# A first pass over 192 instead of 256 prompt tokens, and a second over 96 rows instead of 32

## The chip, the cores and the metric

The kernel runs on one core of one Trainium2 chip, as one program. The metric is device time in microseconds (us), the median over runs.

## The reference, cut to what matters

The kernel computes one step of a decoder layer for 256 prompt tokens and 32 sample tokens (8 sequences of 4). All arithmetic is float32. In short:

```python
qa, ka, va, qb, kc, vc, ks, vs, kw, vw, g = split(x @ w_in)         # 2048 -> 44 tiles of 128 columns, and gates
o_a = stick_breaking(qa, keys, values)                                # 8 heads, samples over 2048 paged positions
kcmp, vcmp = compress(kc, w1_k, w2_k), compress(vc, w1_v, w2_v)        # windows of 32 positions, stride 16
o_c, sel = attend(qb, kcmp, vcmp), top16(importance)                  # compressed branch picks blocks of 64
o_b = g0 * o_c + g1 * attend(qb, selected ks, vs) + g2 * attend(qb, window kw, vw)
h = layer_norm(ALPHA * x + concat(o_a, o_b) @ w_out)                  # w_out 2048 x 2048
q = (h @ w_query).reshape(T, 8 heads, 2, 128); s = q . sub_keys        # w_query 2048 x 2048
experts, gate = top16 of the sums of two top16 lists, softmax          # 128 experts for each token
y = layer_norm(ALPHA * h + sum(gate * gelu(u[expert] . h) * v[expert]))  # rows of 2048 values, gathered
```

Each of the 288 tokens needs 128 rows of `peer_u` and 128 rows of `peer_v`, 8 KB each: 604 MB in all.

## The kernel before, in words

**Three stages.** First, 44 tiles of `w_in` are projected for all tokens, with stick-breaking attention of samples and prompt around it. Then a first pass applies `w_out` to the 256 prompt tokens in two tiles of 128 rows (`out_rows`, L1336), normalises them, turns them (`turn_prompt`, L1347) and applies `w_query` (`query_rows`, L1378; 16 blocks of 128 query columns, with `score_rows`, L1366). Then comes the gather stage, a loop of ticks.

**Slots and groups.** The tokens form 9 groups of 32. A slot is one group with four experts for each token: a gather of 128 rows of `peer_u` (1 MB), a dot product with the replicated `h` on VectorE (`gather_dot`, L2302), a gather of 128 rows of `peer_v`, and four matmuls of 32 output rows each on TensorE (`value_rows`, L1660). There are 288 slots. `slot_group` and `slot_column` say which group and columns a slot has; the first 64 slots alternate groups 0 and 1 (four slots each), the others take a group's 32 slots in one go. The value part of slot s comes 22 ticks later (`LAG`).

**Ticks.** Every engine walks through ticks 0 to 309. At tick t VectorE does `selection(t)`, `background(t)`, then the dot product of slot t; ScalarE does replication, `background(t)`, and the diagonal of slot t-22; TensorE does `background(t)`, then `value_rows(t-22)`; GpSimd issues the `peer_u` gather of slot t and then the `peer_v` gather of slot t-22 (L2410). Both gathers have rings of four buffers, so GpSimd waits for the dot product of slot t-4 and for the matmuls of slot t-26, and for the choice of experts (`chosen`, `CHOSEN_BY`). The first `peer_v` gather also waits until the whole `w_query` pass is over, since its ring holds those weights. Each engine's stream is in order: whatever waits in `background(t)` holds all that follows on that engine. TensorE enters tick 0 only after the last `score` of the first pass.

**The samples' chain** lies in `background`, at ticks written out by hand. Compression: 32 items (`taps`, L1421, 1 MB of pages each, two buffers), three ticks apiece from ticks 20 and 72 (`TAPS_AT`); each pair ends in `cmp_sums` and `cmp_gelu` on VectorE. Picking of blocks from tick 82 (`PICK_AT`), selected and window attention of two halves from 123 and 157 (`NSA_AT`), `w_out` for the 32 samples at 198 to 213 (`OUT_AT`, `out_of`, L1574: four matmuls of 32 rows side by side, then folded), `w_query` for them at 230 to 261 (`QUERY_AT`, `query_of`, L1599: half a block a tick). SyncE loads the weight blocks again for this, 1 MB each, into two of four buffers, each after the block two before it was used. The 1 MB blocks for the items of compression come half from SyncE's queue and half from ScalarE's (`odd_pages`).

**Selection.** The top 16 lists of a head are made on VectorE in three parts (`head_part`), the expert numbers by `experts_head` or `experts_pair`, and `fold` lays them out by slot. First tile at ticks 0 to 44, second at 56 to 104, samples at 240 to 271.

Of the kernel before, what the change touches and what calls it, by code (L numbers as in the profile page):

```python
# [136 lines left out]
TAPS_AT = (20, 72)  # L137
TAPS = {TAPS_AT[kv] + 3 * i + piece: (kv, i, piece) for kv in range(2) for i in range(2 * NB) for piece in range(3)}


def item_ticks(after):

    return {TAPS_AT[kv] + 3 * i + 2 + after: (kv, i) for kv in range(2) for i in range(2 * NB)}


def stage_ticks(after):

    return {TAPS_AT[kv] + 6 * b + 5 + after: (kv, b) for kv in range(2) for b in range(NB)}

# [3 lines left out]
PICK_AT = 82  # L153
NSA_AT = (123, 157)
# [48 lines left out]
CHOSEN_BY = {0: 1, 8: 2, 16: 3, 32: 4, 48: 5, 64: 6, 96: 7, 128: 8, 160: 9, 192: 10, 224: 11, 256: 12, 264: 13, 272: 14, 280: 15}  # L203
# [105 lines left out]
def hybrid_step(nc, dram, outs):  # L309
    stream, later_items = Stream(), Background()  # L310
    with ExitStack() as ctx:
# [175 lines left out]
        vcmp = words(AT_PROJ + 4096, NB, NG * P)  # L487
# [13 lines left out]
        s_cmp = words(AT_PROJ + 3648, 2, P)  # L501
        imp = words(AT_PROJ + 3904, 2, NSEL)
        rank = words(AT_PROJ + 3970, 2, NSEL)
        out_parts = [words(AT_PROJ + 2080 + 512 * k, 512) for k in range(2)]
        p_slc_t = words(AT_H + 4096, NPAGE, P)
# [1986 lines left out]
```

## Time and profile before

| | |
|---|---|
| median of 3 runs | 2566.43 us (2564.66 to 2570.31) |
| the profiled execution | 2569.75 us, of which its span is 2567.9 us |
| TensorE busy | 1892.7 us (74%), mean granted clock 0.811 of 2.4 GHz |
| VectorE busy | 1248.5 us (49%) |
| DMA | 964.23 MB, mean 375 GB/s |
| matmuls of the first pass over `w_out` | 110.1 us (L1336) |
| matmuls of the first pass over `w_query` | 114.2 us (L1378) |

The span runs from the first to the last instruction. "Busy" of TensorE counts modelled ends of pipelined matmuls. One float32 matmul of the program is two MATMUL instructions in the profile. The granted clock is 1.0 at 2.4 GHz and 0.5 at 1.2 GHz.

### The profile page before, as it was taken

To read this page: it belongs to the slowest core of one execution; us is meant where nothing else is said; L and a number is where in the kernel's file an instruction comes from. 1 tells how busy PE (TensorE), PEld (TensorE's weight loads), DVE (VectorE), ACT (ScalarE), POOL (GpSimd) and SP (SyncE) were. 2 spreads that over 40 slices of the span, in tenths; PEclk is the share of its full clock that TensorE was granted. 3 is DMA by queue.
4 is the path that set the end of the run, shared out by engine and by line. 5 is a ranking of instruction groups with operands and counts; after the bars stand their busy time and mean duration, and the time that the engine had idled before them with its cause. 6 is when DMAs were issued, how large, how long until landed. Compare 5 with 4: busy or idle time off the path is not lost.

```text
span 2567.9 us, 29141 instructions
## 1 busy us (share of the span) xinstructions
PE 1892.7 (74%) x9494; PEld 1077.5 (42%) x9494; DVE 1248.5 (49%) x2349; ACT 335.4 (13%) x787; POOL 709.9 (28%) x594
## 2 busy tenths in 40 slices
PE   8999999979999877757777663665553546888345
PEld 5777766544478654434454310221120002655000
DVE  0510122243048867677887535424433345578850
ACT  0000111422031000201100101101110110011011
POOL 0000000000002433333334324323434246334562
PEclk9999999989999998978988885787685655555556
DMA  9889979896349999999999999999999999999998
GB/s 397 301 344 357 371 278 376 339 363 263 121 182 361 391 408 410 408 411 412 409 409 410 410 397 410 409 397 398 415 386 395 421 422 421 421 421 411 419 417 326
DMA packets 213687, 964.23 MB, mean 375 GB/s; under 512 B 23937, under 2 KB 89474, under 8 KB 122818
## 3 DMA queue, kind: packets, MB, share of 16 engines
q0 software_dynamic: 84512, 627.05, 59.7%
q1 hardware_dynamic: 93074, 300.33, 30.6%
q10 hardware_dynamic: 35952, 35.01, 4.0%
q8 instruction: 76, 1.25, 0.2%
q14 instruction: 73, 0.60, 0.1%
HBM read 955.81 MB, written 14.88 MB: 378 GB/s over the span
## 4 chain that ended last, share of the span: by engine, by line
DMA 51%; PE 31%; DVE 9%; issue 4%; SPq 2%; POOL 1%; ACTq 1%; ACT 1%; POOLq 0%; DVEq 0%
DMA sb<-in_peer_u,sb 25%; DMA sb<-in_peer_v,sb 18%; PE bank L1030 14%; DVE sb L2302 5%; PE bank L1336 4%; DMA sb<-in_nsa_t 3%; DMA sb<-in_nsa_v 3%; PE bank L1660 2%; PE bank L1094 2%; PE bank L1134 2%; PE bank L1378 1%; DMA sb<-in_a_v 1%; POOL sb L2410 1%; PE bank L1486 1%; PE bank L1540 1%
## 5 line engine op out<-in xcount | busy, mean ns | idle before, releaser
L1660 PE MATMUL bank<-sb 128*32 128x512 f32 x2304 | 476.5, 848 | 535.6 <-DMA sb<-in_peer_v,sb 513.9
L2302 DVE CUSTOM_DVE_ANT_1 sb<-sb 128x2048 f32<-128x2048 f32 x224 | 513.5, 2293 | 522.5 <-DMA sb<-in_peer_u,sb 520.2
L2410 POOL DMA_INDIRECT sb<-in_peer_v,sb x288 | 400.7, 1391 | 462.5 <-PE bank L1660 380.5
L2410 POOL DMA_INDIRECT sb<-in_peer_u,sb x288 | 301.1, 1046 | 765.6 <-DVE sb L2302 530.5
L1660 PEld LDWEIGHTS bank<-sb 128*32 128x32 f32 x2304 | 63.3, 124 | 754.9 <-DMA sb<-in_peer_v,sb 714.9
L1030 PE MATMUL bank<-sb 128*128 128x288 f32 x1408 | 351.9, 410 | 11.7 <-DMA sb<-in_w_in 11.7
L1030 PEld LDWEIGHTS bank<-sb 128*128 128x128 f32 x1408 | 267.0, 191 | 95.5 <-issue 12.2
L1421 PE MATMUL bank<-sb 128*128 128x256 f32 x1024 | 289.6, 437 | 0.5 <-ACT sb L829 0.5
L1421 PEld LDWEIGHTS bank<-sb 128*128 128x128 f32 x1024 | 249.6, 309 | 79.7 <-issue 62.5
L2302 DVE CUSTOM_DVE_ANT_0 sb<-sb 128x2048 f32<-128x2048 f32 x64 | 146.6, 2294 | 78.6 <-DMA sb<-in_peer_u,sb 74.9
L996 ACT ACTIVATE sb<-sb 128x32 f32<-128x32 f32 x288 | 83.1, 313 | 509.8 <-PE bank L1660 284.8
L2396 POOL DMA_DIRECT2D out_a<-sb x1 | 0.5, 545 | 514.6 <-PE bank L1134 514.6
L1599 PEld LDWEIGHTS bank<-sb 128*128 128x128 f32 x512 | 111.6, 330 | 53.2 <-issue 53.2
L1486 PE MATMUL bank<-sb 128*32 128x512 f32 x128 | 78.9, 777 | 52.8 <-DMA sb<-in_nsa_t 52.8
L1599 PE MATMUL bank<-sb 128*128 128x32 f32 x512 | 116.0, 402 | 0.0
L1378 PE MATMUL bank<-sb 128*128 128x256 f32 (+1 forms) x608 | 114.2, 347 | 1.4 <-issue 0.7
L1336 PE MATMUL bank<-sb 128*128 128x512 f32 x256 | 110.1, 592 | 0.1
L1378 PEld LDWEIGHTS bank<-sb 128*128 128x128 f32 x608 | 99.8, 191 | 11.9 <-issue 0.9
L1540 PE MATMUL bank<-sb 128*32 128x256 f32 x256 | 75.0, 459 | 39.6 <-DMA sb<-in_nsa_v 39.6
L825 ACT ACTIVATE sb<-sb 32x2048 f32<-32x2048 f32 x36 | 68.6, 1906 | 68.2 <-issue 37.1
L667 ACT ACTIVATE sb<-bank 128x288 f32<-128x288 f32 x44 | 18.0, 410 | 440.0 <-PE bank L1030 440.0
L1336 PEld LDWEIGHTS bank<-sb 128*128 128x128 f32 x256 | 48.6, 190 | 61.1 <-issue 60.7
(363 smaller groups left out, 1489.2 us busy)
## 6 DMA issues: line engine op xcount, KB each, us to landing
sb<-in_a_k SPq DMA_DIRECT2D x128, 512.0 KB, 6.7
sb<-in_a_v SPq DMA_DIRECT2D x128, 512.0 KB, 6.8
sb<-in_w_in SPq DMA_DIRECT2D x44, 1024.0 KB, 9.0
sb<-in_w_out SPq DMA_DIRECT2D x32, 1024.0 KB, 8.9
sb<-in_w_query SPq DMA_DIRECT2D x32, 1024.0 KB, 9.1
sb<-in_nsa_t SPq DMA_DIRECT2D x200, 128.0 KB, 9.9
sb<-in_nsa_t ACTq DMA_DIRECT2D x184, 128.0 KB, 14.2
sb<-in_nsa_v SPq DMA_DIRECT2D x64, 128.0 KB, 18.2
```

Source lines behind the costliest of these rows:

```text
L825: act.activation(replica(g)[32 * q:32 * q + 32], src, ACT.Copy).then_inc(rep_in, 1)
L996: act.activation(diag[j % 4], const["fold"], ACT.Copy, scale=w16[:, r % 2, j:j + 1]).then_inc(diag_in, 1)
L1030: mm = pe.matmul(bank[step % 2][:, 0:T], w[:, kt * P:(kt + 1) * P], x_t[:, kt, :], start=(kt == 0), stop=(kt == KT - 1))
L1336: mm = pe.matmul(bank[3 * (n % 2) + tt][:, :], mix(4 * kq + kt)[:, P * tt:P * tt + P], w[:, kt, :], start=(kq == 0 and kt == 0), stop=(kq ...
L1378: mm = pe.matmul(bank[5 if m == 2 else m % 2][:, lo:hi], w[:, P * kt:P * kt + P], h_t[:, kt, lo:hi], start=(kt == 0), stop=(kt == KT - 1), ...
L1421: mm = pe.matmul(bank[(7, 3)[n % 2]][:, 0:256], rows[:, :, l], w1_one[:, :, l, :], start=(l == 0), stop=(l == 15), skip_group_check=True)
L1486: mm = pe.matmul(bank[((5, 6), (7, 2))[ph][c]][32 * b4:32 * b4 + 32, :], q_pad[:, 4 * h + b4, g], rows[:, 4 * c:4 * c + 4, g, :], start=(g ...
L1540: mm = pe.matmul(bank[4][r, 0:256], p_slc_t[:, 8 * ph + j, r], rows[:, 256 * j:256 * j + 256], start=(ph == 0 and j == 0), stop=False, ski ...
L1599: mm = pe.matmul(bank[2 + m % 2][:, 0:NSMP], w[:, P * kt:P * kt + P], h_t[:, kt, NPROMPT:T], start=(kt == 0), stop=(kt == KT - 1))
L1660: mm = pe.matmul(bank[g % 2][32 * c:32 * c + 32, :], diag[j % 4], v_ring[j % 4][:, 512 * c:512 * c + 512], start=(s in FIRST), stop=(s in ...
L2302: dve.tensor_tensor_reduce(out=u, in0=u, in1=replica(g), scale=1.0, scalar=0.0, op0=ALU.mult, op1=ALU.add, accum_out=act16[:, r % 2, j:j + ...
L2410: pool.indirect_dma_start(rows[j % 4], None, dram[table], bass.IndirectOffsetOnAxis(ap=idx, axis=0)).then_inc(full[j % 4], 16)
```

## The change: what it does

- The first pass takes 192 prompt tokens: tile 0 has 128 rows, tile 1 has 64 (`ROWS_1`). In `out_rows` for tile 1 the even and odd products go to rows 0 to 63 and 64 to 127 of the bank, and VectorE adds both. `score_rows` for tile 1 writes rows 64 to 127. `query_rows` streams 192 columns instead of 256.
- The other 64 prompt tokens and the 32 samples are tile 2 of 96 rows. `out_of` makes two products for each of 4 parts of a block, one of 64 rows and one of 32, in one bank; no fold. `query_of` takes a whole block in one tick, with 96 columns.
- Groups 0 to 5 are the first 192 tokens, 6 and 7 the other prompt tokens, 8 the samples. Slots 192 to 255 alternate groups 6 and 7.
- The chain: an item of compression starts every 2.25 ticks on average, from tick 6 on (in two pieces of 8 taps instead of three of 6, 6 and 4), picking at 50, attention at 80 and 114, `w_out` at 154 to 169, `w_query` at 178 to 193. The selection for tile 2 runs at ticks 183 to 218.
- The final norm of prompt tokens is in three parts, and the load of its weights waits for the last block of `w_query`.

```diff
+GROUPS_1 = 6
+ROWS_1 = NSMP * (GROUPS_1 - 4)
+TOK_1 = P + ROWS_1
+ROWS_2 = T - TOK_1
+ROWS_P = NPROMPT - TOK_1
+PARTS_1 = P // ROWS_1
...
-TAPS_AT = (20, 72)
-TAPS = {TAPS_AT[kv] + 3 * i + piece: (kv, i, piece) for kv in range(2) for i in range(2 * NB) for piece in range(3)}
+TAPS_AT = 6
+def taps_tick(kv, i):
+    n = 2 * NB * kv + i
+    return TAPS_AT + 9 * (n // 2) // 2 + 2 * (n % 2)
+TAPS = {taps_tick(kv, i) + piece: (kv, i, piece) for kv in range(2) for i in range(2 * NB) for piece in range(2)}
...
-    return {TAPS_AT[kv] + 6 * b + 5 + after: (kv, b) for kv in range(2) for b in range(NB)}
+    return {taps_tick(kv, 2 * b + 1) + 1 + after: (kv, b) for kv in range(2) for b in range(NB)}
...
-PICK_AT = 82
-NSA_AT = (123, 157)
+PICK_AT = 50
+NSA_AT = (80, 114)
-OUT_AT = 198
-QUERY_AT = 230
+OUT_AT = 154
+QUERY_AT = 178
+REPLICATE.update({192 + q: (7, q) for q in range(4)})
+def shared(s):
+    return s // 64 in (0, 3)
-CHOSEN_BY = {0: 1, 8: 2, 16: 3, 32: 4, 48: 5, 64: 6, 96: 7, 128: 8, 160: 9, 192: 10, 224: 11, 256: 12, 264: 13, 272: 14, 280: 15}
+CHOSEN_BY = {0: 1, 8: 2, 16: 3, 32: 4, 48: 5, 64: 6, 96: 7, 128: 8, 160: 9, 192: 10, 200: 11, 208: 12, 224: 13, 240: 14, 256: 15}
...
             def out_rows(k, tt):
                 n, kq = k // 4, k % 4
                 w = arrived("wo", k).rearrange("p (k c) -> p k c", k=4)
+                parts, rows = (1, P) if tt == 0 else (PARTS_1, ROWS_1)
                 for kt in range(4):
-                    mm = pe.matmul(bank[3 * (n % 2) + tt][:, :], mix(4 * kq + kt)[:, P * tt:P * tt + P], w[:, kt, :],
-                                   start=(kq == 0 and kt == 0), stop=(kq == 3 and kt == 3))
+                    own = slice(rows * (kt % parts), rows * (kt % parts) + rows)
+                    mm = pe.matmul(bank[3 * (n % 2) + tt][own, :], mix(4 * kq + kt)[:, P * tt:P * tt + rows], w[:, kt, :],
+                                   start=(kq == 0 and kt < parts), stop=(kq == 3 and kt >= 4 - parts))
...
-                query_rows(m, 0, NPROMPT).then_inc(item_used, 1)
+                query_rows(m, 0, TOK_1).then_inc(item_used, 1)
...
-                for l in range(6 * piece, min(16, 6 * piece + 6)):
+                for l in range(8 * piece, 8 * piece + 8):
...
                 for kt in range(4):
-                    mm = pe.matmul(bank[2 + n][32 * kt:32 * kt + 32, :], smp_mix_t[:, 4 * kq + kt, :], w[:, kt, :],
-                                   start=(kq == 0), stop=(kq == 3))
+                    at = 4 * kq + kt
+                    first, last = kq == 0 and kt == 0, kq == 3 and kt == 3
+                    pe.matmul(bank[2 + n][0:ROWS_P, :], mix_2[:, at, :], w[:, kt, :], start=first, stop=last, skip_group_check=True)
+                    mm = pe.matmul(bank[2 + n][ROWS_P:ROWS_2, :], smp_mix_t[:, at, :], w[:, kt, :], start=first, stop=last, skip_group_check=True)
...
-            def query_of(m, half):
...
-                for kt in range(8 * half, 8 * half + 8):
-                    mm = pe.matmul(bank[2 + m % 2][:, 0:NSMP], w[:, P * kt:P * kt + P], h_t[:, kt, NPROMPT:T], start=(kt == 0), stop=(kt == KT - 1))
+            def query_of(m):
...
                 for kt in range(KT):
+                    mm = pe.matmul(bank[2 + m % 2][:, 0:ROWS_2], w[:, P * kt:P * kt + P], h_t2[:, kt, :], start=(kt == 0), stop=(kt == KT - 1))
...
-                if 0 <= d < 32:
-                    query_of(d // 2, d % 2)
-                if d >= 5 and d % 2 == 1 and d < 37:
-                    score_of((d - 5) // 2)
+                if 0 <= d < 16:
+                    query_of(d)
+                if 2 <= d < 18:
+                    score_of(d - 2)
```

## Rows read from the trace of the kernel before

**Rows 1.** The page's 40 slices of 64 us: busy tenths, granted clock, rate.
```profile
DVE  0510122243048867677887535424433345578850
PEclk9999999989999998978988885787685655555556
GB/s 397 301 344 357 371 278 376 339 363 263 121 182 361 391 408 410 408 411 412 409 409 410 410 397 410 409 397 398 415 386 395 421 422 421 421 421 411 419 417 326
```

**Rows 2.** Stretches: length, busy of PE, PEld, DVE, ACT, POOL, clock, DMA share, GB/s.
```profile
618.00:728.00 110.00, 110.00 (x257) 48.72 (x258) 13.08 (x28) 2.30 (x3) 1.80 (x3) 1.00 0.44 164
752.00:855.00 103.00, 101.96 (x518) 90.64 (x517) 84.25 (x208) 23.05 (x56) 28.64 (x24) 1.00 0.94 369
870.00:1440.00 570.00, 411.33 (x1928) 273.07 (x1927) 422.82 (x842) 68.76 (x181) 202.52 (x193) 0.89 1.03 410
1320.00:1350.00 30.00, 23.47 (x108) 16.04 (x108) 28.83 (x45) 2.56 (x9) 8.71 (x8) 0.89 1.03 407
1980.00:2070.00 90.00, 44.49 (x196) 7.66 (x196) 29.85 (x36) 8.89 (x18) 22.48 (x24) 0.64 1.01 422
2164.00:2363.00 199.00, 178.63 (x789) 121.02 (x786) 126.94 (x286) 21.81 (x68) 80.68 (x63) 0.50 1.01 421
2500.00:2550.00 50.00, 30.51 (x152) 3.57 (x152) 1.86 (x9) 7.80 (x23) 17.58 (x19) 0.67 1.00 396
```

**Rows 3.** Chain that ended last, 580 to 900 us: start, us, what.
```profile
617.94 110.13 PE bank L1336 x256
```

**Rows 4.** Timeline, end of `w_out` and the start of `w_query`: start, us, engine, line.
```profile
714.45 0.69 DVE L1970 SCALAR_TENSOR_TENSOR sb<-sb,bank 128x512 f32<-128x512 f32 x1 [12.31 <-PE bank L1336]
...
720.87 2.35 DVE L1992 SCALAR_TENSOR_TENSOR sb<-sb 128x2048 f32<-128x2048 f32 x1
...
753.65 3.74 PE L1378 MATMUL bank<-sb 128*128 128x128 f32 x32
...
754.56 1.01 POOL L2410 DMA_INDIRECT sb<-in_peer_u,sb  x1 [134.26 <-DVEq L2090]
...
757.45 7.07 PE L1378 MATMUL bank<-sb 128*128 128x256 f32 x32
...
764.36 0.61 PE L1366 MATMUL bank<-sb 128*128 128x128 f32 x4
```

**Rows 5.** Landing times of weight blocks, 690:752 and 1940:2075: KB, median us.
```profile
sb<-in_w_query SPq DMA_DIRECT2D x5, 1024.0 KB, 4.8
...
sb<-in_w_out SPq DMA_DIRECT2D x14, 1024.0 KB, 9.2
```

**Rows 6.** Timeline of DVE: dot products of slots 0 and 12.
```profile
760.50 2.29 DVE L2302 CUSTOM_DVE_ANT_0 sb<-sb 128x2048 f32<-128x2048 f32 x1 [6.88 <-DMA sb<-in_peer_u,sb]
...
823.25 2.29 DVE L2302 CUSTOM_DVE_ANT_0 sb<-sb 128x2048 f32<-128x2048 f32 x1
```

**Rows 7.** Timelines of POOL and PE where the `peer_v` gathers begin.
```profile
853.03 1.84 POOL L2410 DMA_INDIRECT sb<-in_peer_v,sb  x1 [1.28 <-PE bank L1378]
...
854.48 7.47 PE L1421 MATMUL bank<-sb 128*128 128x256 f32 x32 [0.54 <-ACT sb L829]
861.88 1.06 PE L1660 MATMUL bank<-sb 128*32 128x512 f32 x8
...
868.19 0.71 PE L1433 MATMUL bank<-sb 128*128 128x128 f32 x4
```

**Rows 8.** Timeline of DVE in the ranking of blocks.
```profile
1338.46 1.29 DVE L2167 TENSOR_TENSOR sb<-sb 128x1089 f32<-128x1089 f32 x1
```

**Rows 9.** Timelines of PE in the samples' `w_out` and `w_query`.
```profile
1962.32 1.94 PE L1660 MATMUL bank<-sb 128*32 128x512 f32 x8 [3.05 <-DMA sb<-in_peer_v,sb]
1964.03 1.93 PE L1574 MATMUL bank<-sb 128*32 128x512 f32 x8
...
2184.93 1.93 PE L1660 MATMUL bank<-sb 128*32 128x512 f32 x8 [1.04 <-DMA sb<-in_peer_v,sb]
2186.79 3.62 PE L1599 MATMUL bank<-sb 128*128 128x32 f32 x16
```

More of the change, by code:

```diff
@@ L33, with place @@
 NGRP = T // NSMP
+GROUPS_1 = 6
[4 more added lines that the diff above has]
+PARTS_1 = P // ROWS_1
+def place(g):
+    if g < 4:
+        return 0, slice(32 * g, 32 * g + 32)
+    tile, row = (1, 32 * (g - 4)) if g < GROUPS_1 else (2, 32 * (g - GROUPS_1))
+    return tile, slice(row, row + 32)
 SCALE = 1.0 / float(np.sqrt(HD))
@@ L500, in hybrid_step @@
         o_nsa = words(AT_PROJ + 3392, NG * P)
[L501 to L505, printed above, removed]
+        s_cmp = prompt_vcmp
+        imp = words(AT_SMALL - 4 * NSEL, 2, NSEL)
+        rank = words(AT_SMALL - 2 * NSEL, 2, NSEL)
+        p_slc_t = words(AT_PROJ + 4096, NPAGE, P)
         end_rows = words(AT_T + 4096, 512)
@@ L820, in replicate @@
             def replicate(g, q):
-                if g >= 4:
+                if g == NGRP - 1:
+                    act.wait_ge(later_used, later_items.n)
+                elif g >= 4:
                     act.wait_ge(rep_used, g - 1)
-                src = h_nat[32 * (g % 4):32 * (g % 4) + 32, g // 4, :].rearrange("p (a b) -> p a b", a=KT)
+                tile, own = place(g)
+                src = h_nat[own, tile, :].rearrange("p (a b) -> p a b", a=KT)
                 act.activation(replica(g)[32 * q:32 * q + 32], src, ACT.Copy).then_inc(rep_in, 1)
@@ L976, in background @@
-                if t == 264:
+                if d == 18:
+                    norm_square(ROWS_2, 2, 3, words(AT_PROJ + 4096, DM))
+                elif d == 20:
+                    norm_root(ROWS_2, 2, 3)
+                elif d in (22, 23):
+                    for c in range(2 * d - 44, 2 * d - 42):
+                        turned_second(c)
+                d = t - QUERY_AT
+                if 1 <= d < 17:
+                    m = d - 1
+                    act.wait_ge(later_used, later_items.used["wq", m])
+                    if m >= 2:
+                        act.wait_ge(s_mm, 18 + m - 1)
+                    act.activation(q_t[:, m % 2, 0:ROWS_2], bank[2 + m % 2][:, 0:ROWS_2], ACT.Copy).then_inc(q_in, 1)
@@ L1003, in _ @@
                 background(t)
-                if 17 < t <= SLOTS_ALL + 1 and t % 16 == 1:
+                if 17 <= t <= SLOTS_ALL + 1 and t % 16 == 1:
                     gelu_exp16(t // 16 - 1)
@@ L2058, in second_ranks, with fold @@
                 at = slice(16 * h0, 16 * (h0 + count))
                 keys_of(tt, h0, count, f_b, i_b, 1)
-                ch.do(dve.scalar_tensor_tensor(out=expert_nat[0:n, at], in0=i_a[0:n, at], scalar=float(P), in1=i_b[0:n, at],
+                ch.do(dve.scalar_tensor_tensor(out=expert_nat[r, at], in0=i_a[r, at], scalar=float(P), in1=i_b[r, at],
                                                op0=ALU.mult, op1=ALU.add))
-            def fold(dst, nat, tt, group, cols):
-                own = nat[32 * group:32 * group + 32, 4 * cols.start:4 * cols.stop].rearrange("p (s q) -> p q s", q=4)
+            def fold(dst, nat, g, cols):
+                tile, rows = place(g)
+                at = rows.start + rows_of[tile].start
+                own = nat[at:at + 32, 4 * cols.start:4 * cols.stop].rearrange("p (s q) -> p q s", q=4)
@@ L2067, in fold @@
                 for q in range(4):
-                    dve.tensor_copy(dst[32 * q:32 * q + 32, 4 * tt + group, cols], own[:, q, :]).then_inc(dve_step, 1)
+                    dve.tensor_copy(dst[32 * q:32 * q + 32, g, cols], own[:, q, :]).then_inc(dve_step, 1)
                     ch.n += 1
@@ L2332, in collect @@
                 dve.wait_ge(v_used, LAST_OF[g] + 1)
-                own = slice(32 * (g % 4), 32 * (g % 4) + 32)
-                tt = g // 4
+                tt, own = place(g)
                 for c in range(4):
```

370 lines of the change are left out of this document (183 added, 187 removed).

## The prediction

> **What bounds the kernel now.** I read the page's slices first. The rate of DMA falls to 121 and 182 GB/s in slices 11 and 12 (642 to 770 us) and is near 410 to 422 GB/s in nearly all slices behind, up to the end [rows 1]. So the gather stage is bound by bytes, and the stage before it by something else. The stretches say by what: from 618 to 728 us TensorE is busy all of 110.0 us at full clock with DMA at 164 GB/s; from 752 to 855 it is busy 101.96 of 103.0 us, and DMA is at 369 already [rows 2]. The chain of waits has one piece of 110.13 us of `w_out` matmuls there [rows 3]. From 870 to 1440 us DMA runs at 410 GB/s with TensorE busy 72% and VectorE 74% of the time [rows 2].
>
> From this follows my way of counting. The bytes of the kernel hardly change (both weights are still loaded twice), so the end moves by the DMA time that is no longer idle, less the idle time that is new.
>
> **First pass over `w_out`.** 128 products of 512 columns in 110.13 us are 0.86 us each [rows 3]; a block is 8 of them, 6.88 us. Tile 1 now has 64 rows, with even and odd products side by side. Four products of 32 rows take 1.71 us together at the low clock (from 1962.32 to 1964.03) [rows 9], as much as one alone at that clock (2 x 0.86). No row shows groups of 64. Bounds: they overlap fully, 1.72 instead of 3.44 us a block, or not at all, nothing gained. I take the first, by the rows of 32. A change between narrow and full width costs 0.15 us: the next full matmul comes 1.86 us behind the value rows, the next narrow one 1.71 [rows 9]; two changes a block make 0.3. So a block takes 3.44 + 1.72 + 0.3 = 5.46. The last four blocks do tile 0 first: tile 0 is finished at 618 + 12 x 5.46 + 4 x 3.44 = 697.3, and tile 1 at 704.3. Then VectorE's chain takes 714.45 to 723.22, 8.8 us [rows 4], which before lay beside 13.8 us of tile 1; now it ends at 706.4 and TensorE waits 2 us. The turn starts at 706.6 instead of 728.1: 21.5 us. VectorE's extra additions (0.69 us each [rows 4]) lie beside matmuls. The first four `w_query` blocks land in 4.8 us [rows 5], in time.
>
> **First pass over `w_query`.** A product of 256 columns is 7.07 / 16 = 0.44 us, one of 128 is 3.74 / 16 = 0.23 [rows 4]. With 192 columns I take 0.33, between them. 13 blocks of 16 save 13 x 1.75 = 23 us, less two changes of width for each block's scores, 13 x 0.3 = 4: 19 us. The first three blocks go by parts; 64 columns instead of 128 may save nothing (weights must be loaded) up to half of 3 x 3.74; I take 1 us with the shorter turn. The pass ends near 853 - 21.5 - 19 - 1 = 811.5, 41 us earlier.
>
> **Why that is not the gain.** The first `peer_u` gather, issued at 754.56 [rows 4], comes 22 us earlier, near 732. That is the first credit: 22 us of DMA. From then on the old kernel moved 369 GB/s of a possible 422 up to 855 [rows 2], 103 x (1 - 369/422) = 13 us idle; with blocks used faster beside the same gathers I count 9 of it as removed. Credit so far: 31 us.
>
> Against it stands the tick where the chain now begins. VectorE goes from slot 0 to slot 12 in 62.75 us [rows 6], so it reaches tick 12 near 738 + 63 = 801, bytes permitting. There `cmp_sums(0, 0)` stands in front of dot product 12, and it waits for the turns of items 0 and 1. TensorE enters tick 0 only at 811.5: two items and a half of the third at 7.47 us and two turns at 0.71 [rows 7] end at 831.6. The cause is the order of TensorE's stream, not its speed. Behind the waiting instruction are dot products 12 onward, the choice `chosen` 3 at tick 13 that slot 16 needs, and so all further `peer_u` gathers; and the first `peer_v` gather comes only after the gather of slot 22. Before, GpSimd issued it at 853.03 [rows 7].
>
> How long is DMA idle? From 732 it has to move 12 blocks of `w_query`, 16 slots of `peer_u` (12 and the ring of 4) and 2 items: 30 MiB, 31.5 MB, at 422 GB/s 75 us, to 807. Then only items 2 to 4 can go, about 8 us. Gathers resume when tick 13 is done, near 831.6 + 2.3 + 3.8 = 838 (a dot product and the second half of a choice). Idle: 838 - 807 - 8 = 23 us. Bounds: 10 (VectorE slowed by the fuller DMA, items arriving early) to 35 (item 2 late, ScalarE's half of the pages queued behind its own waits).
>
> A check from the other side: `value_rows(0)` now stands behind 8 items instead of 1: 811.5 + 8 x 7.47 + 7 x 0.71 = 876, with small waits 880, where it was 861.88 [rows 7]. By then 7 more items are done (7.3 MB, 18 us at 408). That is about even, and the four `peer_v` blocks are all in, worth some us more. Both counts give a small gain: by the ledger 31 - 23 = 8 us.
>
> **The denser chain.** An item in 2.25 ticks instead of 3 makes a tick 2.44 MiB, 6.3 us at 408 GB/s. TensorE needs 1.06 + 7.47 / 2.25 + 0.71 / 2.25 = 4.7 us of it [rows 7]. The ranking of blocks (five passes over 33 x 33 pairs of 1.29 us for each half [rows 8], with their place moved to ticks 66 to 69) meets the second tile's selection and `cmp_gelu`: I count 48 us of VectorE in 6 ticks of 38. Four buffers ahead in both rings hide about 20 us of it; the like stretch from 1320 to 1350, VectorE busy 28.8 of 30 us, still had 407 GB/s [rows 2]. Cost 2 us (0 to 8).
>
> **Second pass, `w_out`.** 16 ticks of 3 MiB are 7.5 us at 422. TensorE needs 4 pairs (64 rows beside 32) of 0.86, 3.4 us, and 1.1 for value rows at full clock; twice that, 9.0, at the low one. The clock was 0.64 from 1980 to 2070 with TensorE half busy, 0.89 from 870 to 1440 with it 72% busy [rows 2], so with more work I expect it in between. Buffers: a block lands in 9.2 us [rows 5], plus 3.4 of use is 12.6 of two ticks, 15.
>
> **Second pass, `w_query`.** Each product had 0.226 us an instruction at the low clock with 32 columns (3.62 / 16) [rows 9], more than 32 columns need. 96 columns need 96/128 of a 128-column instruction, 0.09 us at full clock and 0.18 at the low one, so 32 instructions of a block stay at 7.2 us low, about 3.7 full. The low end is a bound for a tick: 7.2 + 1.9 + 0.4 = 9.5 against 7.5, 16 times, 32 us lost; the high end loses nothing. The clock was 0.50 through 2164 to 2363, but 0.67 where value rows ran almost back to back [rows 2]. With three times the columns in half the ticks I take it near 0.7 and 2 us lost for both passes. The selection at ticks 183 to 214 loads VectorE with about 5.1 us a tick where a tick of gathers alone is 5.0: 1 us. What is moved beyond slot 192 (replica of group 7, choices 10 to 12) has two slots of margin by the tick tables.
>
> **Sum.** 31 - 23 - 2 - 2 - 1 = 3, and a rest of about 3 for the `peer_v` blocks found above: 6 us less. The profiled execution took 2569.75 (span 2567.9), so 2563.7; it lies 3.3 above the median, so 2560.4 as the median.
>
> **Rivals.**
> - *Head start kept.* If the stall at tick 12 falls in time that DMA fills otherwise (its lower bound, or VectorE later there than I think), 31 us less 5 remain: 2566.4 - 26 = 2540. For it: TensorE is busy without a break from 618 to 855 [rows 2, 3], and its work shrinks by 41 us. Against it: the order of TensorE's stream.
> - *64 beside 32 does not overlap.* Then `out_of` has 8 products of 0.86, 6.9 us, and 8 changes of width of 0.15, 1.2; with value rows 9.2 us a tick against 7.5: 16 x 1.7 = 27 us. Time 2587, slower. It decides as soon as TensorE's tick passes 7.5 us. For it: the changes between widths are visible [rows 9], and every row with overlap has equal widths.
>  The Trainium skill, "TensorEngine Tiling (Array Packing)", section "Key Properties", says that a change of tiling mode, not just of tile, drains TensorE. By that rule this rival would be right; the 0.15 us agrees with it, but can also be full width waiting for the last narrow group.
> - *Late start.* If items take 10 us instead of 7.5 with two buffers and landings like 9.2 us [rows 5], `value_rows(0)` comes 20 us later, at 900: 2580, slower.
> - *No side by side in the first pass either*: 16 x 1.72 = 27 us less head start: 2584.
>
> **How the numbers follow.** The forecast has a chance of 0.41 (its own range 2550 to 2572), head start kept 0.22, no overlap of 64 and 32 (with TensorE's low clock) 0.20, late start 0.12, the last 0.05. A measurement here tells about 0.2%, 5 us. Faster than 2561.3: 0.22 and 0.25 of the forecast's 0.41, 0.47. Slower than 2571.6: the last three hold 0.37, of which I leave 0.04 to come out within 0.2%: 0.33. Within: those 0.04 and the rest of the forecast, 0.20. The range 2534 to 2590 takes in the bounds of idle (10 to 35) and of overlap, and leaves out 2 in 10, above all both bad cases together.
>
> **What would show it.** Turn of tile 0 near 707; first `peer_u` gather near 732; a gap of some 25 to 30 us in dot products before slot 12, idle DMA at 807 to 838; `value_rows(0)` near 880; 408 GB/s from there. `out_of` at 3.4 us a block at full clock, or about 8. I am wrong if dot product 12 comes without a gap, or if the rate falls under 400 in the two second passes.

## The result and the profile after

The changed kernel takes 2602.32 us (median of 4 runs, 2596.75 to 2605.7) against 2566.07 us (4 runs): ratio 1.0134, interval 1.012 to 1.0147. It is slower by some 36 us, outside the forecast's range. The profiled execution took 2604.48 us, span 2602.6 us, mean granted clock 0.812 (before 2569.75, 2567.9, 0.811).

The page's slices of after, now 65 us each, beside [rows 1]:

```profile
DVE  0500122253274976569777335433245698444660
...
PEclk9999999989999898999777876769978755555556
...
GB/s 402 301 346 357 372 278 357 362 332 268 144 323 215 396 400 399 391 405 351 400 403 417 403 399 411 410 340 421 363 378 422 410 421 421 422 422 422 422 408 323
```

The hole of slices 11 and 12 is narrower, but there is a new one in slice 13 (215 GB/s), and slices 19, 27 and 29 have 351, 340 and 363, where 412, 397 and 415 stood. A slice of 65 us mixes stages, so here are the stretches behind them, in the columns of [rows 2]:

```profile
618.00:704.00 86.00, 85.04 (x253) 30.27 (x251) 13.46 (x30) 2.30 (x3) 0.74 (x2) 1.00 0.50 185
731.00:808.00 77.00, 77.00 (x472) 73.25 (x472) 53.81 (x132) 18.70 (x42) 16.55 (x16) 1.00 0.98 394
808.00:850.00 42.00, 40.86 (x196) 39.84 (x195) 16.44 (x37) 5.02 (x13) 5.25 (x3) 1.00 0.39 123
870.00:1170.00 300.00, 235.25 (x1143) 179.40 (x1142) 209.41 (x426) 34.53 (x98) 120.98 (x92) 0.90 1.02 400
1170.00:1230.00 60.00, 49.42 (x248) 37.34 (x246) 57.22 (x102) 6.34 (x21) 24.85 (x18) 0.94 0.91 345
1770.00:1890.00 120.00, 120.00 (x331) 21.38 (x330) 37.92 (x45) 4.61 (x15) 36.84 (x28) 1.00 0.98 388
...
1765.00:1830.00 65.00, 65.00 (x175) 11.44 (x174) 20.83 (x27) 2.36 (x8) 21.71 (x16) 0.99 1.01 419
1830.00:1905.00 75.00, 75.00 (x221) 13.53 (x221) 20.45 (x25) 2.27 (x8) 19.45 (x16) 1.00 0.96 358
...
1950.00:2540.00 590.00, 268.94 (x1356) 91.65 (x1360) 371.44 (x683) 75.59 (x181) 337.44 (x214) 0.57 1.01 419
```

The `w_out` pass ends at 703.0, 25 us earlier. From 731 to 808 us DMA is nearly full. From 808 to 850 it moves 123 GB/s. In the denser chain it has 400 instead of 410, in the ranking of blocks 345 with VectorE busy 57 of 60 us, in the second `w_out` pass 388 with TensorE busy all the time at full clock: 419 in its first half and 358 in its second. From 1950 to 2540 us it is 419, and next to nothing is lost.

Timelines where the stall was forecast, VectorE and GpSimd first and then TensorE, beside [rows 6, 7]:

```profile
731.66 0.99 POOL L2451 DMA_INDIRECT sb<-in_peer_u,sb  x1 [112.92 <-DVEq L2126]
...
793.47 2.29 DVE L2342 CUSTOM_DVE_ANT_0 sb<-sb 128x2048 f32<-128x2048 f32 x1
...
832.41 0.48 DVE L2161 TENSOR_SCALAR sb<-bank,sb 128x256 f32<-128x256 f32 x1 [32.81 <-PE bank L1462]
834.18 2.29 DVE L2342 CUSTOM_DVE_ANT_0 sb<-sb 128x2048 f32<-128x2048 f32 x1
...
841.38 2.40 POOL L2451 DMA_INDIRECT sb<-in_peer_u,sb  x1 [43.87 <-DVEq L2136]
```

```profile
813.20 11.02 PE L1450 MATMUL bank<-sb 128*128 128x256 f32 x48 [0.66 <-ACT sb L861]
824.05 0.61 PE L1462 MATMUL bank<-sb 128*128 128x128 f32 x4
824.50 7.36 PE L1450 MATMUL bank<-sb 128*128 128x256 f32 x32
831.70 0.61 PE L1462 MATMUL bank<-sb 128*128 128x128 f32 x4
...
856.74 6.12 PE L1450 MATMUL bank<-sb 128*128 128x256 f32 x16 [4.34 <-DMA sb<-in_nsa_t]
...
879.93 6.46 PE L1450 MATMUL bank<-sb 128*128 128x256 f32 x16 [4.91 <-DMA sb<-in_nsa_t]
...
890.40 1.07 PE L1686 MATMUL bank<-sb 128*32 128x512 f32 x8
```

VectorE's first sums (L2161) wait 32.81 us for the second turn (L1462 at 831.70), dot product 12 comes 40.7 us behind dot product 11, and GpSimd issues no gather for 43.87 us. The first value rows (L1686) come at 890.40, where they came at 861.88 [rows 7].

A ledger shows when the time goes. It sums the bytes of all DMA packets in the trace that started before a time, and takes off the sum of the kernel before at the same time (MB; 1 MB is 2.4 us at 422 GB/s). Plus is ahead of the kernel before. It is of one execution each: the same code can differ by 3 MB there. The other rows are variants that the next section explains.

```
                                    808    870   1170   1230   1700   2000 us
changed kernel                     +9.7   -0.3   -3.4   -7.3   -7.8  -12.9
b_first, first passes alone       +11.1  +12.9  +12.9  +12.9  +12.3  +12.9
b_first8, same, items tick 8       +9.4   +2.5   +3.4   +3.3   +3.2   +3.5
b_early, before, items tick 8      +1.5   -6.4   -8.5   -8.3   -8.1   -8.3
b_dense, before, denser chain      +1.0   +1.1   -2.6   -3.3   -4.6   -4.3
a_nr, ranking spread, 3 x 32       +9.7   -0.1   -3.2   -3.9   -6.1   -3.6
a_t8, same, items tick 8          +10.0   +4.1   +0.1   -0.6   -4.0   -0.6
```

The head start is there at 808 us and gone at 870. The rest goes later: up to 1170 us, from 1170 to 1230 and from 1700 to 2000.

### The profile page after: what moved, and what is told of

Read it like the earlier page. It is cut to its first block, busy times and chain, and to the rows that moved or that the text cites. A ratio compares the mean times of both kernels' runs of the same rounds, so it can differ in the third digit from the quotient of the medians.

```text
span 2602.6 us, 29438 instructions
## 1 busy us (share of the span) xinstructions
PE 1868.9 (72%) x9614; PEld 1022.1 (39%) x9614; DVE 1270.4 (49%) x2409; ACT 341.5 (13%) x789; POOL 816.4 (31%) x595
## 2 busy tenths in 40 slices
DMA packets 213849, 965.31 MB, mean 371 GB/s; under 512 B 23969, under 2 KB 89506, under 8 KB 122850
## 3 DMA queue, kind: packets, MB, share of 16 engines
q1 hardware_dynamic: 93282, 301.90, 30.5%
## 4 chain that ended last, share of the span: by engine, by line
PE 47%; DMA 35%; DVE 7%; issue 4%; ACTq 3%; ACT 1%; SPq 1%; POOL 1%; POOLq 0%; DVEq 0%
DMA sb<-in_peer_v,sb 18%; PE bank L1055 13%; DMA sb<-in_nsa_t 8%; PE bank L1450 7%; PE bank L1686 4%; PE bank L1407 3%; PE bank L1363 3%; DMA sb<-in_peer_u,sb 3%; DMA sb<-in_nsa_v 3%; DMA sb<-in_w_query 3%; PE bank L1605 2%; DVE sb L2342 2%; PE bank L1606 2%; PE bank L1119 2%; PE bank L1159 2%
## 5 line engine op out<-in xcount | busy, mean ns | idle before, releaser
L1686 PE MATMUL bank<-sb 128*32 128x512 f32 x2304 | 479.1, 831 | 494.1 <-DMA sb<-in_peer_v,sb 434.4
L2451 POOL DMA_INDIRECT sb<-in_peer_v,sb x288 | 495.5, 1720 | 681.4 <-PE bank L1686 589.3
L2451 POOL DMA_INDIRECT sb<-in_peer_u,sb x288 | 312.6, 1085 | 478.0 <-DVE sb L2342 229.0
L1686 PEld LDWEIGHTS bank<-sb 128*32 128x32 f32 x2304 | 66.4, 124 | 769.0 <-DMA sb<-in_peer_v,sb 659.3
L1450 PE MATMUL bank<-sb 128*128 128x256 f32 x1024 | 268.1, 421 | 60.0 <-DMA sb<-in_nsa_t 54.1
L1055 PEld LDWEIGHTS bank<-sb 128*128 128x128 f32 x1408 | 266.4, 191 | 95.2 <-issue 12.2
L1450 PEld LDWEIGHTS bank<-sb 128*128 128x128 f32 x1024 | 244.3, 309 | 92.4 <-DMA sb<-in_nsa_t 66.6
L1515 PE MATMUL bank<-sb 128*32 128x512 f32 x128 | 74.4, 751 | 61.7 <-DMA sb<-in_nsa_t 61.7
L1627 PE MATMUL bank<-sb 128*128 128x96 f32 x512 | 78.2, 325 | 24.9 <-DMA sb<-in_w_query 24.9
L1407 PE MATMUL bank<-sb 128*128 128x192 f32 (+2 forms) x608 | 93.3, 312 | 1.2 <-issue 0.7
L1627 PEld LDWEIGHTS bank<-sb 128*128 128x128 f32 x512 | 75.6, 238 | 39.7 <-DMA sb<-in_w_query 31.3
L1407 PEld LDWEIGHTS bank<-sb 128*128 128x128 f32 x608 | 89.0, 190 | 4.0 <-ACT sb L883 2.1
L1363 PE MATMUL bank<-sb 128*64 128x512 f32 (+1 forms) x256 | 87.0, 603 | 0.1
L1159 PE MATMUL bank<-sb 128*32 128x512 f32 x512 | 67.8, 663 | 7.6 <-DMA sb<-in_a_v 7.6
```

The source lines that it names most:

```text
L1055: mm = pe.matmul(bank[step % 2][:, 0:T], w[:, kt * P:(kt + 1) * P], x_t[:, kt, :], start=(kt == 0), stop=(kt == KT - 1))
L1159: mm = pe.matmul(bank[(0 if half else 6) + c][r, :], z_t[:, half, 2 * pp + j, r], rows[b4][:, 1024 * j + 512 * c:1024 * j + 512 * c + 512] ...
L1363: mm = pe.matmul(bank[3 * (n % 2) + tt][own, :], mix(4 * kq + kt)[:, P * tt:P * tt + rows], w[:, kt, :], start=(kq == 0 and kt < parts), s ...
L1407: mm = pe.matmul(bank[5 if m == 2 else m % 2][:, lo:hi], w[:, P * kt:P * kt + P], h_t[:, kt, lo:hi], start=(kt == 0), stop=(kt == KT - 1), ...
L1450: mm = pe.matmul(bank[(7, 3)[n % 2]][:, 0:256], rows[:, :, l], w1_one[:, :, l, :], start=(l == 0), stop=(l == 15), skip_group_check=True)
L1515: mm = pe.matmul(bank[((5, 6), (7, 2))[ph][c]][32 * b4:32 * b4 + 32, :], q_pad[:, 4 * h + b4, g], rows[:, 4 * c:4 * c + 4, g, :], start=(g ...
```

## The experiments

Times are medians; ratios are against the kernel before on the same chip (2565.14 to 2567.57 us). Names with b_ are variants of the kernel before, names with a_ variants of the changed kernel.

### The start of the items

**b_early**: the kernel before, items of the first half from tick 8.

```diff
-TAPS_AT = (20, 72)
+TAPS_AT = (8, 72)
```

> The kernel before with one number changed: the first 16 items of compression start at tick 8 instead of 20 (cmp_sums for the first pair stands at tick 16 instead of 28), all else at its old tick. Theory (order of TensorE's stream): VectorE reaches tick 16 near 840 us, TensorE leaves the w_query pass near 854 and needs 2.5 items, so dot product 16 stalls until about 874; some 20 to 25 us of DMA stay idle, and since nothing else is moved earlier they come back only in part: 12 to 25 us slower than before (2578 to 2591), with a gap of over 25 us in front of dot product 16. Rival (an early start is harmless, since the bytes of the items are moved ahead): within 5 us of before and a rate above 380 GB/s from 840 to 875.

Measured 2592.08 us, ratio 1.0099 (1.0082 to 1.0115). VectorE waits there as in the changed kernel:

```profile
832.75 2.29 DVE L2302 CUSTOM_DVE_ANT_0 sb<-sb 128x2048 f32<-128x2048 f32 x1
...
869.04 0.48 DVE L2127 TENSOR_SCALAR sb<-bank,sb 128x256 f32<-128x256 f32 x1 [33.37 <-PE bank L1433]
```

The place of the items alone costs 27 us, a little over what was expected. The rival, that an early start is harmless, falls.

**b_first, b_first14, b_first8**: the kernel before with the shorter first passes, items from tick 20, 14 and 8. They leave out the work for the last 64 prompt tokens.

```diff
+                parts, rows = (1, P) if tt == 0 else (2, 64)
...
+                    own = slice(rows * (kt % parts), rows * (kt % parts) + rows)
-                    mm = pe.matmul(bank[3 * (n % 2) + tt][:, :], mix(4 * kq + kt)[:, P * tt:P * tt + P], w[:, kt, :],
+                    mm = pe.matmul(bank[3 * (n % 2) + tt][own, :], mix(4 * kq + kt)[:, P * tt:P * tt + rows], w[:, kt, :],
...
-                query_rows(m, 0, NPROMPT).then_inc(item_used, 1)
+                query_rows(m, 0, P + 64).then_inc(item_used, 1)
```

> The kernel before with nothing but the shorter first passes: w_out and w_query work for 192 prompt tokens, tile 1 of w_out as pairs of 64 rows side by side; items, choice of pages, attention and second passes stay at their ticks (items from tick 20). It leaves out the work for the last 64 prompt tokens, whose scores are then stale values, so its output is not the reference's. Theory (the head start is 27 us of bytes at 808 us, but behind it VectorE's 5 us a tick with one MiB of peer_u a tick moves half of what DMA can, until slot 22): a rate near 210 to 300 GB/s from 812 to 850 us, 10 to 15 us kept, 2552 to 2558 us. Rival 1 (all of the head start is kept where no item stands in front of VectorE): 2538 to 2542 us. Rival 2 (none is kept: peer_v can't begin sooner): 2565 to 2569 us.

> The kernel as in the run before it (first passes for 192 prompt tokens, the rest of their work left out, so not the reference's output), with the items of the first half from tick 14 instead of 20. Theory (items fill what DMA has left before slot 22; the first sums stand at tick 22, where VectorE arrives near 845 us, and TensorE has turned the first two items by 832): no wait of VectorE over 5 us, 2542 to 2550 us. Rival (any earlier item costs, as with the kernel before and items from tick 8, 27 us for 12 ticks, by holding up value rows behind items): 2560 to 2575 us.

> The kernel before with the first passes for 192 prompt tokens (the rest of their work left out, so not the reference's output) and its items from tick 8 instead of 20. Theory (head start and early items are separate: the first is worth 27 us, items 12 ticks earlier cost 27 us wherever the pass ends, as both are set by what TensorE does in order before its first value rows): 2562 to 2570 us, value rows of slot 0 near 855 us. Rival (only the time from VectorE's arrival at the first sums, tick 16 near 811 us, to the second turn near 832 us counts): 2550 to 2557 us.

```
items from tick   first value rows   median    ratio (interval)
20                832.6 us           2539.94   0.9897 (0.9881 to 0.9912)
14                862.0 us           2547.36   0.9916 (0.9902 to 0.9929)
 8                864.5 us           2559.44   0.9973 (0.9962 to 0.9984)
```

At tick 20 rival 1 was right and my theory of VectorE's pace wrong: all 27 us are kept. The stretch 810 to 840 us in the run from tick 20 and in the run from tick 8:

```profile
810.00:840.00 30.00, 17.46 (x68) 13.02 (x68) 28.83 (x65) 2.71 (x11) 18.49 (x12) 0.72 0.96 377
```

```profile
810.00:840.00 30.00, 25.54 (x115) 24.09 (x114) 7.83 (x20) 2.03 (x8) 5.46 (x4) 0.89 0.55 192
```

VectorE is busy 28.8 us in the one and 7.8 in the other, where its first sums wait 22.73 us. The time of the run from tick 14 is in its theory's range, but not for its reason: that theory had no wait over 5 us. Dot product 22 came 21.2 us behind dot product 21, and for 15.41 us of it VectorE waited for a turn. TensorE's own wait is seen there; the turn (L1435) stands behind the next item's first part, which waits for pages:

```profile
834.39 4.69 PE L1423 MATMUL bank<-sb 128*128 128x256 f32 x20
851.44 5.49 PE L1423 MATMUL bank<-sb 128*128 128x256 f32 x12 [12.37 <-DMA sb<-in_nsa_t]
856.73 0.84 PE L1435 MATMUL bank<-sb 128*128 128x128 f32 x4
```

From tick 8 the items cost 19.5 us behind the shorter passes and 27 behind the long ones. That lies between the two theories of b_first8: head start and place of the items are not quite separate.

### Moving the stall

**a_late**: items from tick 12, one every 2 ticks. **a_shift**: items stay, the steps behind them come later.

```diff
-    return TAPS_AT + 9 * (n // 2) // 2 + 2 * (n % 2)
+    return (12, 46)[kv] + 2 * i
...
-PICK_AT = 50
+PICK_AT = 53
```

```diff
-    return {taps_tick(kv, 2 * b + 1) + 1 + after: (kv, b) for kv in range(2) for b in range(NB)}
+    return {max(taps_tick(kv, 2 * b + 1) + 1, 14 + 4 * (NB * kv + b)) + after: (kv, b) for kv in range(2) for b in range(NB)}
```

> The changed kernel with the items of compression at ticks 12, 14, ... 42 and 46, 48, ... 76 instead of from tick 6 at 2.25 ticks each, and picking at 53 instead of 50; everything from attention on as in the changed kernel. The first cmp_sums stands at tick 18 instead of 12. Theory (order of TensorE's stream): the gap before dot product 12 (40.7 us) goes, a small one of under 12 us may stand before slot 18, and 10 to 22 us of the 36 come back (2580 to 2592). Rival (the loss at 808 to 850 us comes from too few bytes to move at the end of the w_query pass, or the denser items cost as much later): 2598 to 2608.

> The changed kernel; TensorE still starts the items at tick 6, but the steps behind each pair of items (sums, exponential, gelu, second product) come later where VectorE would have to wait: the first sums at tick 17 instead of 12, then one pair every 4 ticks until the old places are reached at pair 9. Theory (the idle DMA at 808 to 850 us comes from VectorE waiting at tick 12 for turns that TensorE can't finish before 832): the gap of 41 us before dot product 12 goes, some 10 us of wait stand before tick 17 instead, dot product 24 comes near 868 to 875 us instead of 890.7, and the kernel takes 2582 to 2592 us. Rival (the pace in this stretch is set by TensorE's items and by the two page buffers, whatever VectorE does; the wait only moves): the waits reappear in ticks 17 to 40, 2598 to 2606 us.

a_late: 2606.89 us, ratio 1.018 (1.0151 to 1.0208). a_shift: 2635.39 us, 1.0271 (1.0257 to 1.0284). Neither theory's gain came; a_late lies in its rival's range. In a_late the gap before dot product 12 is gone (797.6 us), but one of 21.9 us stands before dot product 18, and the 7.0 MB still ahead at 840 us are 1.3 MB behind at 1000. Its items also come closer, every 2 ticks instead of 2.25; no run tells that from the later start. a_shift is slower than even its rival said. Its timeline, ScalarE and VectorE:

```profile
860.23 0.38 ACT L894 ACTIVATE sb<-bank 128x256 f32<-128x256 f32 x1 [8.81 <-PE bank L1450]
...
864.49 0.21 ACT L846 ACTIVATE sb<-sb 128x16 f32<-128x16 f32 x1 [3.88 <-issue]
...
864.80 0.17 DVE L2365 TENSOR_SCALAR sb<-sb 128x16 f32<-128x16 f32 x1 [20.83 <-ACT sb L846]
```

VectorE waits 17.7 us at tick 17, then 20.83 us at tick 18 for a small exponential (L846) that stands in ScalarE's order behind its copies of items (L894), which wait for TensorE; and TensorE waits 16.6 us for the delayed sums before it may turn the next item. So the tick ties three engines together: with the steps behind the items moved, VectorE, ScalarE and TensorE each waited for another.

### The denser chain

**b_dense**: the kernel before, items from tick 20 with the changed kernel's spacing.

```diff
+    return TAPS_AT[0] + 9 * (n // 2) // 2 + 2 * (n % 2)
...
-                for l in range(6 * piece, min(16, 6 * piece + 6)):
+                for l in range(8 * piece, 8 * piece + 8):
```

> The kernel before; its items start at tick 20 as ever, but come in 2.25 ticks instead of 3 and in two pieces, so that the chain of the second half ends some 28 ticks earlier; choice of pages, attention and second passes stay where they were. Theory (the denser chain alone loses 7 us, since two page buffers and VectorE's waits for turns no longer fit into a tick): rate 390 to 400 GB/s instead of 410 in the chain, 2569 to 2575 us. Rival (the density costs nothing by itself; what the changed kernel loses there comes from its early start with a full backlog): 2563 to 2567 us.

Measured 2578.29 us (6 runs), ratio 1.004 (1.0026 to 1.0054): 10.7 us, above the range of the theory; the rival falls. Its stretch, which had 410 GB/s in [rows 2]. Then waits from 850 to 1170 us (in all, times, longest): of b_dense, of the changed kernel and of the kernel before.

```profile
870.00:1440.00 570.00, 406.52 (x1918) 275.29 (x1917) 421.02 (x845) 69.45 (x187) 245.00 (x185) 0.81 1.01 400
```

```profile
DVE sb L2135 <- PE bank L1441: 58.0, 9, 11.8
...
PE bank L1429 <- DMA sb<-in_nsa_t: 37.4, 9, 8.3
```

```profile
DVE sb L2161 <- PE bank L1462: 64.4, 10, 12.5
...
PE bank L1450 <- DMA sb<-in_nsa_t: 46.0, 12, 7.4
```

```profile
PE bank L1660 <- DMA sb<-in_peer_v,sb: 88.9, 48, 8.5
DVE sb L2302 <- DMA sb<-in_peer_u,sb: 78.5, 41, 5.1
```

L1441 and L1462 are turns, L1429 and L1450 items, L1660 value rows and L2302 dot products. With the denser chain TensorE waits for pages and VectorE for turns, in b_dense as in the changed kernel. In the kernel before VectorE waits for no turn there, and TensorE's weight loads wait 2.6 us for pages. Both engines wait for gathered rows instead: there the gathers set the pace.

### Ranking and second w_out pass

**a_rank** spreads the ranking over ticks 65, 68, 71, 77, 80. **a_narrow** splits the 64 prompt rows into two products of 32 columns. **a_wide** widens the samples' product to 64 columns instead. **a_nr** has a_rank and a_narrow.

```diff
-                elif d in (16, 18):
-                    pick_above((d - 16) // 2)
...
+                elif s in (65, 71):
+                    pick_above((65, 71).index(s))
...
```

```diff
-                    pe.matmul(bank[2 + n][0:ROWS_P, :], mix_2[:, at, :], w[:, kt, :], start=first, stop=last, skip_group_check=True)
+                    for r in (0, 32):
+                        pe.matmul(bank[2 + n][r:r + 32, :], mix_2[:, at, r:r + 32], w[:, kt, :], start=first, stop=last, skip_group_check=True)
```

```diff
-                    mm = pe.matmul(bank[2 + n][ROWS_P:ROWS_2, :], smp_mix_t[:, at, :], w[:, kt, :], start=first, stop=last, skip_group_check=True)
+                    mm = pe.matmul(bank[2 + n][ROWS_P:P, :], x_t[:, at, PTOK - 32:T], w[:, kt, :], start=first, stop=last, skip_group_check=True)
```

> The changed kernel with the four ranking steps of the blocks on VectorE at ticks 65, 68, 71 and 77 and the last at 80, instead of 66 to 70. Theory (VectorE overloaded in six ticks costs DMA time because slots, not bytes, are late): the rate of 302 GB/s from 1200 to 1230 us goes back above 380 and 5 to 10 us come back (2592 to 2597). Rival (the dip comes from something else in that stretch, or what it gives is given back to the attention stage): within 3 us of 2602.

> The changed kernel with the 64 prompt rows of out_of as two products of 32 rows, so that each of the four parts of a block has three products of 32 rows side by side instead of one of 64 and one of 32. Theory (a product of 64 and one of 32 rows don't overlap, each change of width waits): a block takes 3.4 to 3.6 us instead of 7.9, the rate from 1770 to 1890 stays near 420, and 8 to 14 us come back (2588 to 2594). Rival (these ticks are held by landing of the blocks in two buffers and not by TensorE): a block gets shorter but the time stays within 4 us of 2602.

> The changed kernel; in the second w_out pass the product of the samples' 32 rows is widened to 64 stationary columns (32 of them not meant for it, so what the samples get is not the reference's), beside the 64 prompt rows. Theory (only products of unequal width fail to overlap): a block takes near 3.5 to 4.5 us at full clock instead of 7.9, the rate at 1770 to 1920 us rises to 420 GB/s, 2592 to 2598 us like the variant with three products of 32 columns. Rival (two products overlap only where they are 32 columns wide, or where both come out of one tile, as in the first pass): the block stays near 7 to 8 us, 2600 to 2604 us.

> The changed kernel with two edits: the 64 prompt rows of the second w_out pass as two products of 32 columns, and the ranking of blocks spread over ticks 65 to 80. Theory (both losses are stretches of their own and add up): 7 + 7 us less than 2602, 2584 to 2590 us. Rival (the second is covered by the first, since both only move the same backlog): 2593 to 2597 us.

```
           median    ratio (interval)            less than 2602.32
a_rank     2594.91   1.0107 (1.009 to 1.0124)     7.4
a_narrow   2595.45   1.0115 (1.0098 to 1.0132)    6.9
a_wide     2593.49   1.0101 (1.0088 to 1.0114)    8.8
a_nr       2582.19   1.0054 (1.0041 to 1.0068)   20.1
```

One by one these prices are rough. The runs of a_rank (2588.49 to 2600.0 us) and a_narrow (2593.84 to 2603.23) overlap with those of the changed kernel, and the traced execution of a_narrow is its slowest. Those of a_wide (up to 2596.14) and a_nr (up to 2586.33) do not.

The ranking stretch of a_rank has 401 GB/s where the changed kernel had 345:

```profile
1170.00:1230.00 60.00, 52.71 (x248) 39.48 (x248) 50.56 (x93) 5.36 (x18) 19.09 (x18) 0.88 1.02 401
```

TensorE in the second `w_out` pass of the changed kernel, then of a_narrow with its stretch, then of a_wide:

```profile
1820.88 1.07 PE L1605 MATMUL bank<-sb 128*64 128x512 f32 x2
1821.88 1.05 PE L1606 MATMUL bank<-sb 128*32 128x512 f32 x2
1822.85 1.07 PE L1605 MATMUL bank<-sb 128*64 128x512 f32 x2
```

```profile
1812.61 0.60 PE L1606 MATMUL bank<-sb 128*32 128x512 f32 x2
1812.62 0.59 PE L1607 MATMUL bank<-sb 128*32 128x512 f32 x1
1813.04 0.60 PE L1606 MATMUL bank<-sb 128*32 128x512 f32 x2
```

```profile
1770.00:1890.00 120.00, 89.94 (x520) 21.34 (x512) 42.17 (x47) 5.14 (x17) 41.13 (x34) 0.82 1.01 421
```

```profile
1821.58 0.59 PE L1605 MATMUL bank<-sb 128*64 128x512 f32 x1
1821.59 0.59 PE L1606 MATMUL bank<-sb 128*64 128x512 f32 x1
1822.01 0.59 PE L1605 MATMUL bank<-sb 128*64 128x512 f32 x1
```

64 beside 32 columns: each product starts when the other is done, 1.00 and 0.97 us behind it, so a block takes 7.9 us. Three of 32 start together, and so do two of 64; a step is 0.43 us, two steps a product, a block 3.4 us at full clock. So it is the unequal width that keeps them apart, and not 64 columns as such. The stretch goes from 388 to 421 GB/s. Together the two edits give 20 us, 6 more than their sum, which is about the scatter of one kernel's runs (9 us in the changed kernel); both theories of a_nr named a smaller gain.

### Towards a better version

**a_nrs** is a_nr with a_shift's edit, **a_t6** a_nr with each turn one tick earlier, **a_t8** the same with items from tick 8 (ranking at 67 to 80).

The first of these lines is in a_t8 alone, the second in a_t6 and a_t8:

```diff
-TAPS_AT = 6
+TAPS_AT = 8
...
-CMP_ROWS, CMP_TURN = item_ticks(1), item_ticks(2)
+CMP_ROWS, CMP_TURN = item_ticks(1), item_ticks(1)
```

> The changed kernel with three edits together: the 64 prompt rows of the second w_out pass as two products of 32 columns, the ranking of blocks spread over ticks 65 to 80, and the later steps behind the items as in the variant above. Theory (the losses are separate stretches of idle DMA and add up): 7 + 7 + 10 to 20 us less than 2602, so 2566 to 2580 us, with about 3 MB of the 12 MB of lag left at 2000 us. Rival (one loss hides another: what is saved early is waited for again in front of the next full stretch of VectorE): 2585 to 2592 us.

> The changed kernel with both of these edits (ranking at ticks 67 to 80), items from tick 8 instead of 6, and each item's turn placed one tick earlier in TensorE's order, in front of the next item's first half. Theory (VectorE's wait in front of the first sums is what costs: it arrives at tick 14 near 807 us, and the turns are done near 828 instead of 832): a gap of 20 to 25 us instead of 41, 8 to 10 us less than the kernel with the two edits alone, 2574 to 2582 us. Rival (the wait only moves on to the next sums and to ScalarE's copies, as in the variants with later steps): 2585 to 2595 us.

> The changed kernel with the two products of 32 columns, the ranking at ticks 65 to 80, and each item's turn one tick earlier in TensorE's order; items still from tick 6. Theory (a turn that stands behind the next item's first half waits for that item's pages as well, in the dense chain above all): the gap before dot product 12 goes from 41 to 37 us, fewer waits behind it, 2575 to 2580 us. Rival (the turn's place is nothing, what helped the variant from tick 8 was its two ticks): 2580 to 2585 us.

a_nrs: 2613.31 us, ratio 1.0184 (1.017 to 1.0198), 31 us over a_nr, as a_shift is 33 over the changed kernel: both expectations missed, because both counted the shift as no loss. a_t6: 2580.68 us, 1.0054 (1.0042 to 1.0067), not told apart from a_nr; the turn's place is worth nothing that can be measured. a_t8: 2575.48 us (11 runs), 1.0027 (1.0018 to 1.0036), in its theory's range, but by 6.7 us under a_nr where 8 to 10 were expected. Against a_t6, from which it differs by the two ticks of the items and of some ranking steps, that is worth 5 us. Its wait at the first sums:

```profile
827.62 0.48 DVE L2162 TENSOR_SCALAR sb<-bank,sb 128x256 f32<-128x256 f32 x1 [22.44 <-PE bank L1462]
```

Of the versions that do all the work none beats the kernel before; a_t8 wins back 27 of the 36 us.

## Why the prediction was wrong

- **First pass over `w_out`: right.** Pairs of 64 rows overlap. Tile 0's last addition begins at 696.13 us (TensorE through with tile 0 by then, forecast 697.3), the turn starts at 704.95 (706.6).
- **First pass over `w_query`: right.** It ends near 812.5 (811.5); the first `peer_u` gather is issued at 731.66 (732). The credit of 31 us was of the right size: b_first, which keeps the items at tick 20, has it by the ledger (12.9 MB, 30.6 us) and 26.7 us of it by the medians. That its 2539.94 us meet the 2540 of the rival "head start kept" is luck: the rival took 5 us off for the denser chain and the second passes, which b_first does not have.
- **The stall at tick 12: right in place and cause, a little too small.** Turns done at 832 (831.6), next gather at 841.4 (838). From 808 to 850 us DMA moves 123 GB/s, which against 422 is 30 us idle (forecast 23, bounds 10 to 35). The ledger, which stands at -0.4 MB at 850 us, loses 10.1 MB there, 24 us: the kernel before lost 6 us in that stretch too. The gap of 40.7 us was named as 25 to 30; GpSimd's 43.87 are no price, since DMA had other work for a part.
- **`value_rows(0)` at 880: 10 us too early.** It came at 890.4: the eight items took 77.2 us, 9.6 each, with 4.34 and 4.91 us for pages in two of them. Half of the rival "late start". The rest of 3 us for `peer_v` was not there: at 850 us the changed kernel is 0.9 us behind, where I counted 8 us ahead. Of that the larger stall is 7 us.
- **The denser chain at 2 us: the step that failed most.** I compared TensorE's mean of 4.7 us with a tick of 6.3 and took four slots of buffer as cover. The mean hides that an item comes whole: pages, item, copy, turn and sums follow one another through two buffers. b_dense prices it at 10.7 us and a_rank the ranking at 7.4; together 18 us, as the changed kernel loses from 850 to 1700 us, and the bound of 8 was too low. The slots of cover were not there either: from 850 to 1170 us VectorE waits 78.5 us for gathered rows in the kernel before and 9.4 us in the changed one, so there the gathers are no longer ahead of the engines. I read 407 GB/s at 1320 to 1350 us [rows 2] as proof that a full VectorE costs nothing; but near it, from 1300 to 1360 us, TensorE still waited 14.9 us for gathered rows, and in the changed kernel's ranking it does not.
- **64 beside 32 rows: wrong way round.** The rival "64 beside 32 does not overlap" was right: 7.9 us a block where it said 8.1. The rule of the Trainium skill cited there, "TensorEngine Tiling (Array Packing)", "Key Properties", is that a change of tiling mode drains TensorE. The trace agrees: 1.00 us a product instead of 0.86. The price was not 27 us: a_wide and a_narrow give 7 to 9, with a_rank beside it up to 13, and the ledger of the changed kernel loses 5.1 MB, 12 us, from 1700 to 2000 us. TensorE's tick was 8.8 us at full clock, near the 9.2 of the rival, but DMA kept 419 GB/s up to 1830 us and fell to 358 only behind that. Three MiB in 8.8 us are 359 GB/s, so only the second half of the pass was held by TensorE. That gathers already issued filled the first half is my reading, which no run shows.
- **Second `w_query` pass, selection, moved choices: right at about nothing.** 419 GB/s from 1950 to 2540 us.
- **Two slips that decided nothing.** The rival without side by side gives 2584, where 2560.4 + 27 is 2587. And [rows 2] leave out 728 to 752 us, so they do not show TensorE busy without a break from 618 to 855: from 720 to 750 us it was busy 28.08 of 30.
- **Not counted:** 1.1 MB more (965.31 against 964.23), 2.6 us at 422 GB/s.

By the times at which both traced executions have moved the same bytes, the changed kernel is behind by 0.9 us at 850, 8.1 at 1170, 18.0 at 1230, 19.6 at 1700, 30.5 at 2000 and 31.9 at 2540 us; the bytes added make about 34.5, and the spans differ by 34.7. By the timed runs, added up: -26.7 for the first passes, +19.5 for items from tick 8, +5.2 for the two ticks more, +10.7 for the density, +20.1 for ranking and unequal width, +2.6 for bytes: 31.4 of 36.3 us. The missing 5 us are within the scatter; that eight items instead of five stand before the first value rows may hold some of it, which no run shows alone. The sum also takes a_narrow's and a_rank's edits, which were timed in the changed kernel, and the density, which was timed in the kernel before, as independent of each other.

The direction came out wrong because three terms of the sum were small numbers taken at their good end: 2 us for the denser chain, 2 for the second passes and 3 of gain for `peer_v`, which measured 18, about 10 and 0; and the 8 us of credit less stall were used up as well.

## What to carry to other kernels

Where engines run through one list of ticks in order, ask of a step that is moved earlier which engine reaches that tick last; its arrival is the price. Here, to keep that step early and move only the steps behind it made the waits longer (a_shift, 33 us). A mean load per tick below the tick's time does not show that a chain of dependent steps through two buffers fits. Give products that are to run side by side on TensorE the same width, even if that means more of them.

## What was not expected of the hardware

- Three products of 32 columns take 0.43 us a step together, one of 64 and one of 32 columns 1.00 and 0.97 us a product after one another. More and narrower instructions took 3.4 us a block instead of 7.9.
- The freed time comes back only in part: in a_narrow TensorE is busy 89.94 of 120 us and is granted 0.82, where the changed kernel, busy throughout, had 1.00. From 1790 to 1795 us, behind a wait for a weight block, a_narrow was granted 0.50, and a step took 0.86 us instead of 0.43.
- In the kernel before, from 870 to 1440 us, pieces of pages of 128 KB landed in 9.9 us (SyncE's queue) and 14.0 us (ScalarE's), beside the gathers. A weight block of 1024 KB took 9.2 us beside gathers and 4.8 us before they began [rows 5]. The piece of an eighth of the size was no faster.
